# Expert slabs loaded in halves in some pairs, the first weight slab loaded alone, and the logits copied inside the root

## The reference

```python
h2 = (rms_norm_2(x, norm2_g[l]) * (1.0 + sc2) + sh2).reshape(B_ * S_, D)
idx, gates = route(h2, router_w, router_b)
y = moe(h2, idx, gates, w_gate[l], w_up[l], w_down[l]).reshape(B_, S_, D)
x = x + gt2 * y
```

```python
def expert_block(args):
    toks, gts, e = args
    xb = h_pad[toks]
    u = jax.nn.silu(xb @ w_gate[e]) * (xb @ w_up[e])
    return (u @ w_down[e]) * gts[:, None].astype(xb.dtype)
```

## Time and profile before

| | us |
|---|---|
| median of 3 runs (lowest, highest) | 2301.04 (2298.81, 2301.11) |
| the profiled execution | 2299.09 |
| its span | 2297.3 |
| TensorE busy | 2188.7 (95%) |
| VectorE busy | 833.0 (36%) |
| ScalarE busy | 346.3 (15%) |
| HBM read | 621.01 MB |

### The profile page before, as it was taken

One profiled execution on the slowest core, in us unless ns is written; L12 is line 12 of the kernel. 1 busy time (PEld: TensorE's weight loads), 2 busy tenths in 40 slices (PEclk: granted clock), 3 DMA queues, 4 the chain that ended last, 5 costly groups with the idle time before them and its releaser, 6 DMA issues.

```text
span 2297.3 us, 26225 instructions
## 1 busy us (share of the span) xinstructions
PE 2188.7 (95%) x10442; PEld 1396.2 (61%) x10442; DVE 833.0 (36%) x1889; ACT 346.3 (15%) x657; POOL 21.9 (1%) x28
## 2 busy tenths in 40 slices
PE   8999999999999999999999989889999999888898
PEld 5666668888888888767644333333657654333333
DVE  2443433344322344344463222222355443222223
ACT  1222221000100000123211111111224111111110
POOL 0000000000000000000000000000000000000000
PEclk9999999999999999999999999999999999999999
DMA  7333344777345577432279999999742399999997
GB/s 295 120 111 121 142 150 190 284 283 278 140 150 209 209 286 267 151 116 108 100 287 407 428 429 429 428 429 427 277 147 74 147 367 425 428 429 429 428 429 301
DMA packets 100518, 623.28 MB, mean 271 GB/s; under 512 B 5200, under 2 KB 7504, under 8 KB 72528
## 3 DMA queue, kind: packets, MB, share of 16 engines
q1 hardware_dynamic: 86752, 566.68, 61.2%
q0 software_dynamic: 12672, 50.33, 5.9%
q10 hardware_dynamic: 1008, 5.07, 0.6%
HBM read 621.01 MB, written 1.05 MB: 271 GB/s over the span
## 4 chain that ended last, share of the span: by engine, by line
PE 75%; DMA 20%; DVE 2%; ACT 1%; issue 1%; SPq 0%; DVEq 0%
DMA ring<-in_w_up 20%; PE ps L1868 14%; PE ps L2406 13%; PE ps L1945 11%; PE ps L1905 10%; PE ps L2112 5%; PE ps L2105 3%; PE ps L2436 3%; PE ps L2256 2%; PE ps L2393 1%; PE ps L2417 1%; PE ps L1978 1%; PE ps L1999 1%; PE ps L1915 1%; PE ps L1968 1%; PE ps L2208 1%
## 5 line engine op out<-in xcount | busy, mean ns | idle before, releaser
L2406 PE MATMUL ps<-ring,hT 128*64 128x512 f32 x1984 | 458.0, 616 | 69.8 <-DMA ring<-in_w_up 55.6
L2406 PEld LDWEIGHTS ps<-ring,hT 128*64 128x64 f32 x1984 | 159.1, 141 | 358.6 <-issue 354.5
L1868 PE MATMUL ps<-hT,ring 128*128 128x256 f32 x1408 | 310.6, 381 | 3.6 <-ACT tmp L649 2.4
L1868 PEld LDWEIGHTS ps<-hT,ring 128*128 128x128 f32 x1408 | 267.2, 191 | 41.3 <-issue 3.1
L1945 PE MATMUL ps<-ring,hT 128*128 128x384 f32 x768 | 259.6, 492 | 2.8 <-DMA ring<-in_a_wqkv 2.8
L2436 PE MATMUL ps<-ring,arena 128*64 128x512 f32 x1024 | 226.8, 595 | 1.4 <-ACT arena L953 1.4
L1905 PE MATMUL ps<-arena,ring 128*128 128x256 f32 x1024 | 225.5, 379 | 0.0
L1905 PEld LDWEIGHTS ps<-arena,ring 128*128 128x128 f32 x1024 | 192.4, 189 | 27.2
L1945 PEld LDWEIGHTS ps<-ring,hT 128*128 128x128 f32 x768 | 143.9, 192 | 95.9 <-DMA ring<-in_a_wqkv 3.7
L2436 PEld LDWEIGHTS ps<-ring,arena 128*64 128x64 f32 x1024 | 70.7, 137 | 139.7 <-issue 137.9
L1170 DVE SCALAR_TENSOR_TENSOR arena<-arena,small 128x512 f32<-128x512 f32 x168 | 126.4, 752 | 6.0
(11 more groups left out here) (380 smaller groups left out, 1827.1 us busy)
## 6 DMA issues: line engine op xcount, KB each, us to landing
ring<-in_w_up SPq DMA_DIRECT2D x64, 2048.0 KB, 17.1
ring<-in_w_down SPq DMA_DIRECT2D x64, 2048.0 KB, 15.7
ring<-in_w_gate SPq DMA_DIRECT2D x60, 2048.0 KB, 17.1
ring<-in_mlp_w SPq DMA_DIRECT2D x32, 2048.0 KB, 8.9
arena<-in_w_mod POOLq DMA_DIRECT2D x24, 2048.0 KB, 10.0
ring<-in_a_wqkv SPq DMA_DIRECT2D x24, 1536.0 KB, 6.5
ring<-in_w_in SPq DMA_DIRECT2D x12, 2048.0 KB, 8.3
ring<-in_b_win SPq DMA_DIRECT2D x6, 2048.0 KB, 7.9
```

The costliest lines, as they stand in the source:

```text
L1868: e = te.matmul(out[:, j, :], w[:, k, c0 + 128 * j:c0 + 128 * j + 128], src[:, k, :], start=(k == order[0]), stop=(k == order[-1]))
L2406: e = te.matmul(bank(b)[SB * h:SB * h + SB], xg[:, P * k + SB * h:P * k + SB * h + SB], slabs.tile(n + h).rearrange("p (k n) -> p k n", k= ...
```

## The change

- `halves` loads two slabs in four DMAs: the first half of each, then the second half of each. A first half waits until TensorE has used the first half of the old slab (`half_freed`), where that one was halved, else for all of it; a second half waits for all of it. It is used for pair 0's up and down, for pairs 1 to 3 and for the last pair. The loop's pairs are loaded whole as before.
- TensorE waits for first halves before k = 0 and for the rest before k = 4 (`part`), or k = 0 and 2 (`down`). In `down`, k is now the outer loop and o the inner, in all pairs.
- SP waits until slab 0 has landed before it issues slab 1. ScalarE issues `const_a` after slab 0 has landed and `xT` after slab 2.
- The mean, the seed and the first Newton iteration stand before the copy of the logits, two iterations behind it. `FILL` is 8 instead of 7, and one more fill stands behind the ranks.

```diff
-FILL = 7
+FILL = 8
...
+    def wait_half_landed(self, eng, n):
+        eng.wait_ge(self.half_landed[n % SLOTS], halved_in_slot(n) * 16)
+
+    def wait_half_done(self, eng, n):
+        if is_halved(n):
+            eng.wait_ge(self.half_done, halved_until(n))
+        else:
+            self.wait_done(eng, n)
...
                     load(n, ring.tile(n)[:, 0:KD * WIDTH_A], a_wqkv[c, w])
+                    if n == A_QKV:
+                        ring.wait_landed(sp, n)
...
+                def halves(n, w, experts):
+
+                    for m, e in enumerate(experts):
+                        ring.wait_half_done(sp, n + m - SLOTS)
+                        sp.dma_start(ring.tile(n + m)[:, 0:HALF], pick(w, e)[:, 0:HALF]
+                                     ).then_inc(half_landed[(n + m) % SLOTS], 16)
+                    for m, e in enumerate(experts):
+                        load(n + m, ring.tile(n + m)[:, HALF:SLAB], pick(w, e)[:, HALF:SLAB])
...
-                    pair(at + PAIR_1 + 6 * (q - 1), [lay * E + 2 * q + m for m in range(2)])
+                    halved_pair(at + PAIR_1 + 6 * (q - 1), [lay * E + 2 * q + m for m in range(2)])
...
-                pair(at + LAST, [lay * E + E - 2 + m for m in range(2)])
+                halved_pair(at + LAST, [lay * E + E - 2 + m for m in range(2)])
...
-                if p == 1:
-                    act.dma_start(const_a[:, :], const_a_d).then_inc(const_a_in, 16)
+            ring.wait_landed(act, A_QKV)
+            act.dma_start(const_a[:, :], const_a_d).then_inc(const_a_in, 16)
+            ring.wait_landed(act, A_QKV + 2)
             act.dma_start(xT, x_d).then_inc(x_in, 16)
...
+                token_mean(lay * 2 + (FIRST_NORM + 1), 5)
+                rsqrt_seed(tok_root, tok_mean)
+                newton(tok_root, tok_t, tok_mean, 1)
                 dve.wait_ge(t_logits, lay + 1)
                 ve.tensor_copy(logits[0:E], bank(6)[0:E, 0:S]).then_inc(t_copied, 1)
-                token_mean(lay * 2 + (FIRST_NORM + 1), 5)
-                rsqrt(tok_root, tok_t, tok_mean)
+                newton(tok_root, tok_t, tok_mean, 2)
...
+                fill(1, 4)
                 pe.wait_ge(first_ready, lay + 1)
...
+                        if halved and k % 4 == 0:
+                            landed_half(slabs, n, m, k == 4)
...
+                            if halved and k == 3:
+                                e.then_inc(slabs.half_done, 1)
...
-                    for o in range(2):
-                        for k in range(4):
+                    for k in range(4):
+                        if halved and k % 2 == 0:
+                            landed_half(slabs, n, m, k == 2)
+                        for o in range(2):
```

More of the change, by code:

```diff
@@ L134, with is_halved, halved_until, halved_in_slot @@
 LOOP_STEPS = 6
+def is_halved(n):
+    return any(lay * LAYER + a <= n < lay * LAYER + b for lay in range(DEPTH) for a, b in ((MOE, LOOPED), (LAST, LAST + 6)))
+def halved_until(n):
+    return sum(is_halved(m) for m in range(n + 1))
+def halved_in_slot(n):
+    return sum(is_halved(m) for m in range(n % SLOTS, n + 1, SLOTS))
 class Ring:
-    def __init__(self, slots, landed, done, credit=0):
+    def __init__(self, slots, landed, done, credit=0, half_landed=None, half_done=None):
         self.slots, self.landed, self.done, self.credit = slots, landed, done, credit
+        self.half_landed, self.half_done = half_landed, half_done
     def tile(self, n):
@@ L389, in program @@
     slab_done = sem("slab_done")
-    ring = Ring(ring_sb, landed, slab_done)
+    half_landed = [sem(f"half_landed_{i}") for i in range(SLOTS)]
+    half_freed = sem("half_freed")
+    ring = Ring(ring_sb, landed, slab_done, 0, half_landed, half_freed)
     over_landed = [sem(f"over_landed_{i}") for i in range(SLOTS)]
@@ L557, in pair, with halved_pair @@
                             load(n + 2 * part + m, ring.tile(n + 2 * part + m), pick(w, e), turns)
+                def halved_pair(n, experts):
+                    for part, w in enumerate((wg, wu, wd)):
+                        halves(n + 2 * part, w, experts)
                 def expert_of(b):
@@ L572, in _ @@
                 for part, w in ((1, wu), (2, wd)):
-                    for m in range(2):
-                        load(at + MOE + 2 * part - 2 + m, ring.tile(at + MOE + 2 * part - 2 + m), pick(w, lay * E + m))
+                    halves(at + MOE + 2 * part - 2, w, [lay * E + m for m in range(2)])
                 ring.wait_done(sp, at + WOUT + 1)
@@ L2398, in scatter, with landed_half, landed_whole, part @@
                         e.then_inc(scattered, 1)
-                def part(b, slabs, n, turns=0, m=2):
+                def landed_half(slabs, n, m, second):
+                    for h in range(m):
+                        if second:
+                            slabs.wait_landed(pe, n + h)
+                        else:
+                            slabs.wait_half_landed(pe, n + h)
+                def landed_whole(slabs, n, turns, m):
                     for h in range(m):
                         slabs.wait_landed(pe, n + h, turns)
+                def part(b, slabs, n, turns=0, m=2, halved=False):
+                    if not halved:
+                        landed_whole(slabs, n, turns, m)
                     for k in range(KD):
+                        if halved and k % 4 == 0:
+                            landed_half(slabs, n, m, k == 4)
                         for h in range(m):
@@ L2426, in turn, with down @@
                     e.then_inc(ue_turned, 1)
-                def down(slabs, n, pair, turns=0, m=2):
+                def down(slabs, n, pair, turns=0, m=2, halved=False):
                     pe.wait_ge(ue_copied, pair + 2)
-                    for h in range(m):
-                        slabs.wait_landed(pe, n + h, turns)
-                    for o in range(2):
-                        for k in range(4):
+                    if not halved:
+                        landed_whole(slabs, n, turns, m)
+                    for k in range(4):
+                        if halved and k % 2 == 0:
+                            landed_half(slabs, n, m, k == 2)
+                        for o in range(2):
                             for h in range(m):
@@ L2451, in expert_pair @@
                         piece(fed)
-                    part(5, slabs, n + m, turns, m)
+                    part(5, slabs, n + m, turns, m, halved)
                     if fed == 1:
@@ L2460, in expert_pair @@
                         pe.wait_ge(xs_copied_v, lay * PIECES + fed + 1)
-                    down(slabs, n + 2 * m, pair, turns, m)
+                    down(slabs, n + 2 * m, pair, turns, m, halved)
                 def clear_out():
@@ L2516, in _ @@
                     pe.wait_ge(t_picked, lay + 2)
-                expert_pair(ring, at + LAST, base + PAIRS, copies + PAIRS + 1)
+                expert_pair(ring, at + LAST, base + PAIRS, copies + PAIRS + 1, halved=True)
                 scatter(base + PAIRS, pairs=True)
```

21 lines of the change are left out of this document (14 added, 7 removed).

## The result

| | before | after |
|---|---|---|
| median (lowest, highest) | 2301.07 (2298.81, 2303.31), 4 runs | 2287.36 (2286.63, 2288.87), 4 runs |
| ratio, 95% interval | 1 | 0.9941 (0.9924 to 0.9958) |
| the profiled execution, its span | 2299.09, 2297.3 | 2287.54, 2285.7 |

The account below looks back on a forecast made before the run. TensorE was taken to set the pace until pair 4's end in each layer, then the expert slabs. Gains 3.9 + 4.0 + 4.6 + 2.3 = 14.8 off 2299.09 gave 2284.3, as median 2286.3; range 2279.5 to 2294.

Parts of the forecast that it names:

- Start, 3.9 forecast: First product: slab 0 lands at 12.4, 2.1 us gained, plus 1.8 us from the clock; bounds 1.2 and 4.6.
- the bound of 3.7 us behind x: Start: slab 0 moves only after x and lands 3.7 us behind its last quarter, at 13.3.
- The clock's 1.8 us: First product: with TensorE's gap down to 0.8 us the clock does not drop, 7.12 becoming 5.33 us.
- the drop moves to another product instead of going: Stated sign of being wrong: the low clock shifts to a different product rather than disappearing.
- ScalarE's stay behind slab 2: Start: ScalarE waits until 25, covered by some 3 us before TensorE needs it at 28.4; reaching TensorE would show error.
- Routing, 2.0 per layer forecast: Logits copied between root steps: ranks 0.5 us earlier, gather 1.45 us faster at full clock; bounds 0.5 and 2.1.
- Halves in pairs 0 to 3, 2.3 forecast: Earlier half loads cut the slab backlog, a lead reaching the layer's end: 2.3 us per layer, bounds 0 and 3.2.
- its bound of 3.2 us: Pair 4's down slabs: most backlog removable per layer, from 11.1 us issue to landing down to an empty queue's 7.9.
- Halves in the last pair, 2.3 forecast: Last pair's up product loses its slab waits, 1.01 us in layer 0 and 1.31 in layer 1; bounds 0 and 2.3.
- The clock does not follow: Rival at start and routing: low clock stays, 5.7 us less gain; chance 0.24 together with the lead failing.
- The gapless stream: Rival in the expert pairs: slabs land without gaps, 10.5 us gained per layer, 2270; chance 0.09 with all upper bounds together.
- That halved transfers cost more: Rival on halved slabs: slower kernel, lead gone beyond 5.5 us per halved slab, some 2460 at 10.9; chance 0.05.

Follow-up runs that it names:

- The last set: Final timings: kernel before 2299.29 us; changed kernel unedited 2287.66; changed kernel with pair 4 halved 2283.05, pairs 4 to 6 halved 2289.84, pair 4 halved plus start fill 2285.98.
- the start part: Kernel before with only SP's wait for slab 0 and ScalarE's later const_a and xT issues: 2297.10 us, ratio 0.9991.
- the first set: First timing of the kernel before, 2301.07 us, and of the full change, 2287.36 us, 4 runs each.

## Why the prediction was right, and where only the sum was

**Start, 3.9 forecast.** Slab 0 at 12.4 was too early. In eight traces with the change's start (one of them with the added start fill; the one without SP's wait is left out) TensorE takes slab 0 at 12.09 to 13.75, mean 12.7; in five with the old start at 12.93 to 14.49, mean 13.7. So the landing is worth 0.9 and not 2.1: the bound of 3.7 us behind x, set aside in the forecast, is what the three traces read for it show (3.67, 3.69 and 3.78). By the rule of the Trainium skill that the forecast cited ("DMA: Bandwidth & Descriptors", section "Queues, rings and completion order"), holding back slabs of the same queue buys nothing: the trace without SP's wait agrees, 3.78 against 3.69.

The clock's 1.8 us is the step that failed, by the sign that the forecast itself named: the drop moves to another product instead of going. That a shorter wait keeps the clock up is true of the first product alone. Counting both it and the products behind it (7.12 for 5.43, 4.34 for 3.63, 17.42 or more for the 16.0 of the one trace with no low clock), an execution loses 0, 1.5 or 3.1 us up to 40 us. With the old start it was 3.1 in three traces of five, with the new one in three of eight. The last set's two traces show the loss moving, not going. The means differ by some 0.5, too little in so few traces to say that the edit changed it.

Another sign of being wrong that the forecast named came true in one trace. It gave ScalarE's stay behind slab 2 a cover of 3 us. In the second trace with pair 4 halved, the one with no low clock here, ScalarE left its wait for the slab and began its first copy at 25.76, and TensorE, early this time, waited for the second:

```profile
21.11 5.41 PE L2002 MATMUL ps<-ring,hT 128*128 128x384 f32 x16
27.09 10.56 PE L2002 MATMUL ps<-ring,hT 128*128 128x384 f32 x32 [0.57 <-ACT arena L741]
```

So a faster start runs into the wait that holds back xT, and 0.57 us of what the clock gave went there.

**Routing, 2.0 per layer forecast.** The second group of logits before:

```profile
1142.50 1.05 PE L2354 MATMUL ps<-xT,arena 128*32 128x256 f32 x4
```

From there to the mask's instruction it was 11.00 us, and is 10.08 (1140.09 to 1150.17); to the gather it is 0.79 less (13.50 and 12.71), where 0.5 was forecast. The fill behind the ranks works in every trace: without it five gathers of eight took 5.3 to 5.5 us, with it none of twenty did, all 3.84. Since three of eight were free of the dip anyway, it is worth 1.0 on average and not 1.45. Here the loss did not move to a product close by: from pair 0's first product to pair 4's gate it takes 115.1 us in all traces. Together 1.8.

**Halves in pairs 0 to 3, 2.3 forecast.** The pair of profiled executions gave 2.3 and 3.1, but the kernel before was slow there, so that this agreement is luck. From pair 4's gate to pair 5's up, ten stretches in traces with whole slabs take 34.6 to 36.3 us, mean 35.3; ten with halves in pairs 0 to 3 take 33.3 to 34.4, mean 33.8: 1.5 per layer. The mechanism is the one forecast. The backlog, from issue to landing of pair 4's first down slab, is 9.8 to 11.5 us in the ten stretches with whole slabs, mean 10.5, and 7.7 to 9.6 with halves, mean 8.9. From pair 5's up to pair 14's it is 264.3 and 264.4 us (1312.20 to 1576.47 before, 1305.24 to 1569.63 after), so the lead reaches the end.

The size was off because the forecast took its bound of 3.2 us from one trace, whose 11.1 lies above the mean; from 10.5 to an empty queue's 7.9 there are 2.6, and of these 1.7 went. What keeps the rest may be that a stream of halves is 1.4% slower, which the forecast set at nothing: 16 halved slabs of 4.9 us lose 1.1 us by that, an estimate that no run separated. The loops of `down` cost nothing either way, as forecast: it takes 7.09 us in both orders. The table of the Trainium skill ("DMA: Bandwidth & Descriptors", section "Bandwidth"), from which the forecast estimated 12.3 us for a halved slab, had the sign and not the size: transfers of 1 MB that queue behind each other moved at 421 GB/s, which is 5.0 us for two.

That not all gaps went shows in the windows of the change and of pair 4 halved (us, busy time and count of each engine, granted clock, DMA share, GB/s):

```profile
1270.00:1290.00 20.00, 20.00 (x96) 8.55 (x94) 8.00 (x14) 3.07 (x5) 0.00 (x0) 1.00 0.97 399
```
```profile
1270.00:1290.00 20.00, 20.00 (x96) 8.54 (x94) 8.64 (x16) 3.06 (x5) 0.00 (x0) 1.00 1.02 427
```

The change's stream still breaks where pair 4's whole slabs begin, 399 GB/s; with pair 4 halved it does not. Six such stretches take 32.4 to 33.4, mean 32.8. Behind that point a slab lands 18 to 22 us after its issue, and two more halved pairs only cost.

**Halves in the last pair, 2.3 forecast.** Where neither pair 14's up product nor the last pair is at the low clock, gate and up together took 15.19 us in layer 0 and take 13.96. But the wait that halves remove depends on the product before. In layer 0 of the start part's trace, with whole slabs, pair 14's up product is low (8.78), and the last pair comes late enough to find its slabs there:

```profile
1596.89 13.96 PE L2409 MATMUL ps<-ring,hT 128*64 128x512 f32 x64 [0.84 <-DVEq L1365]
```

From pair 14's up product to the last down product it is 40.97 us there, and 40.97 too with halves and the same dip (1567.76 to 1608.73): no gain. Over five traces with whole slabs and eight with halves (without the one with fills at the branch) that stretch falls from 41.0 to 40.8 in layer 0 and from 41.6 to 39.1 in layer 1: 2.8 in all, near the forecast, but not as one wait per layer.

**Sum.** Start 0.9, with 0.5 for the clock by the means of the traces; routing 3.6; halves 3.0; last pair 2.8: 10.8. Measured were 13.7 in the first set and 11.6 in the last (2299.29 to 2287.66), so 0.8 to 2.9 us stand in no term. Between the two profiled executions the 11.6 of the spans arose so: 2.4 up to layer 0's logits, 2.2 in its routing, 2.3 up to pair 5, then 2.3 lost in two dips up to the last down product, 0.1 up to layer 1's logits, 2.4 in its routing, 3.1 up to pair 5, and 1.4 at the end. The forecast's terms are 4.0 too high together (2.5 of the start, 1.6 of the lead, 0.4 of the routing, less 0.5 of the last pair). The range has room for that; that the median comes within 1.1 us of 2286.3 is luck, since dips that moved, mostly in its favour, made up for most of the error.

**The rivals.** "The clock does not follow" was true of the start and false of the routing. The gapless stream came partly, and only with pair 4 halved. That halved transfers cost more is true at 5.0 us per slab (4.9 and 1.4%) and not at the 5.5 from which it would decide.

## What to carry to other kernels

Split transfers only where the queue runs dry: halves let the next load be issued earlier, which pays while the queue is short, and cost 1.4% of the stream once it is deep. Try the split one pair past the point where waits for slabs begin, and compare: it gave the best version here (2283.1 us), though only a third of its lead is the split, and two pairs further cost 6.8 us.

Fill an idle gap of TensorE only where nothing that others wait for stands behind the fill: behind the ranks it gave 1.0 us per layer on average, ahead of the last pair three of them delayed it by 2.2 and 1.4 us.

Take no term from the clock or a wait of one trace. Read a part's worth from the stretch between two landmarks, over several traces: two executions of the changed kernel took slab 0 1.66 us apart, and the backlog that the forecast read was 0.6 us above the mean of its kind.

## What was not expected of the hardware

The low clock behaves like a loss that moves. In 13 of 14 traces it stands somewhere between 12 and 40 us (granted clock 0.50, the 1.2 GHz level). In five it is on the first product already, where TensorE had been idle for 2.01 to 2.85 us before it; in the other nine TensorE had been idle for 1.68 us or less, and the clock fell behind the first product or, in one, not at all. That one has a low stretch at 388 to 391 us (granted clock 0.50) that no other trace has.

Further on the same shows in two stretches of equal work. From the product at 40 us to the second group of layer 0's logits it takes 1100.0 us in five traces and 1101.2 to 1102.2 in nine. From layer 0's last down product to the same logits of layer 1 it takes 189.8 to 189.9 in nine and 191.0 to 191.2 in five, where the granted clock is 0.50 for longer. With the last pair halved and no fill ahead of it, the four traces without a dip in layer 0's last pair (13.96) are among the five, and the four with it (15.65) among the nine: 1.2 of the 1.7 us come back behind the pair.

In the loop of expert pairs it costs nothing. Timeline of TensorE in the second trace of the change:

```profile
1334.92 7.09 PE L2476 MATMUL ps<-ring,hT 128*64 128x512 f32 x32 [2.61 <-DMA ring<-in_w_up]
...
1354.50 7.09 PE L2476 MATMUL ps<-ring,hT 128*64 128x512 f32 x32 [1.38 <-DMA ring<-in_w_gate]
1364.30 8.78 PE L2476 MATMUL ps<-ring,hT 128*64 128x512 f32 x32 [2.71 <-DMA ring<-in_w_up]
...
1393.65 7.09 PE L2476 MATMUL ps<-ring,hT 128*64 128x512 f32 x32 [2.60 <-DMA ring<-in_w_up]
```

After an up product of 7.09 us the next gate waits 1.38 for its slab; after one of 8.78 it does not wait, and the next up is on time all the same (29.38 and 29.35 us from up to up). Only where TensorE sets the pace is the low clock paid: at the start, in the gather, and from pair 14's up to the layer's end. There it recurs at the same place in both traces of the change and is absent from the last pair in both traces of the version with pair 4 halved; what sets the place stays open.
